# Experts: the fourth gated product's turn, cast and split, placed ahead of the third pair's down-products and of the next block's first weight half

## What is computed

```python
def clamped_swiglu(g, u):
    g = jnp.minimum(g, SWIGLU_LIMIT)
    u = jnp.clip(u, -SWIGLU_LIMIT, SWIGLU_LIMIT)
    return g * jax.nn.sigmoid(SWIGLU_ALPHA * g) * (u + 1)

def expert_block(args):
    xb, e = args                       # 128 rows of one expert
    hid = xb @ w1[e] + b1[e]           # 1024 -> 2 x 1024
    return clamped_swiglu(hid[:, :D_FF_3], hid[:, D_FF_3:]) @ w2[e] + b2[e]

ys = lax.map(expert_block, (xs, blk_e)).reshape(-1, D)
```

## Time and profile before

| what | value |
|---|---|
| median of 3 runs | 3641.12 us (3632.57 to 3645.83) |
| span of the profiled execution | 3646.2 us |
| busy, share of the span | TensorE 90%, its weight loads 69%, VectorE 62%, ScalarE 43%, GpSimd 7% |
| expert blocks | about 2443 us to 3600 us of the span |

### The profile page before, as it was taken

One profiled execution on the slowest core, in us unless ns is written; L12 is line 12 of the kernel. 1 busy time (PEld: TensorE's weight loads), 2 busy tenths in 40 slices (PEclk: granted clock), 3 DMA queues, 4 the chain that ended last, 5 costly groups with the idle time before them and its releaser, 6 DMA issues. The chain is left out here.

```text
span 3646.2 us, 47903 instructions
## 1 busy us (share of the span) xinstructions
PE 3284.8 (90%) x17130; PEld 2526.6 (69%) x17130; DVE 2265.7 (62%) x2932; ACT 1553.7 (43%) x1964; POOL 266.3 (7%) x194
## 2 busy tenths in 40 slices
PE   7888999999988878899987877869999999999996
PEld 5655787875447557788755655758888888888885
DVE  4375666335703264554445474468888888888885
ACT  1263332010012641200123053247777777777773
POOL 0000000000000000000000000002122212122211
PEclk9889999999989887899988988979999999999997
DMA  5411222232112000122273201069999999999994
GB/s 163 155 30 35 92 92 90 95 93 93 69 36 68 14 1 11 61 95 95 84 283 118 81 5 40 28 254 409 399 373 381 371 381 371 383 368 384 368 385 164
DMA packets 170827, 639.66 MB, mean 175 GB/s; under 512 B 13242, under 2 KB 89146, under 8 KB 113875
## 3 DMA queue, kind: packets, MB, share of 16 engines
q1 hardware_dynamic: 160434, 599.53, 43.6%
q0 software_dynamic: 9648, 35.13, 3.6%
q10 hardware_dynamic: 624, 3.35, 0.2%
HBM read 610.12 MB, written 30.46 MB: 176 GB/s over the span
## 5 line engine op out<-in xcount | busy, mean ns | idle before, releaser
L500 DVE TENSOR_TENSOR experts_rest<-experts_weights,experts_leading 128x2048 fp32r<-128x2048 f32 x386 | 879.2, 2285 | 87.2 <-ACT experts_leading L3118 85.8
L3118 ACT CAST experts_leading<-experts_weights 128x2048 fp32r<-128x2048 f32 x387 | 728.5, 1904 | 31.0 <-PEq L3108 16.9
L506 PE MATMUL psum<-experts_leading,experts_xT_leading 128*128 128x512 f32 x1024 | 402.7, 393 | 7.7 <-DVE experts_rest L500 7.7
L507 PE MATMUL psum<-experts_rest,experts_xT_leading 128*128 128x512 f32 x1024 | 404.7, 395 | 0.0
L508 PE MATMUL psum<-experts_leading,experts_xT_rest 128*128 128x512 f32 x1024 | 403.2, 394 | 0.0
L506 PEld LDWEIGHTS psum<-experts_leading,experts_xT_leading 128*128 128x128 f32 x1024 | 192.9, 188 | 52.6 <-DVE experts_rest L500 8.1
L507 PEld LDWEIGHTS psum<-experts_rest,experts_xT_leading 128*128 128x128 f32 x1024 | 193.1, 189 | 44.6
L508 PEld LDWEIGHTS psum<-experts_leading,experts_xT_rest 128*128 128x128 f32 x1024 | 193.0, 188 | 43.4
L506 PE MATMUL psum<-experts_leading,experts_hidden_leading 128*128 128x512 f32 x512 | 211.4, 413 | 3.4 <-DVE experts_hidden_rest L3204 3.3
L507 PE MATMUL psum<-experts_rest,experts_hidden_leading 128*128 128x512 f32 x512 | 201.4, 393 | 0.0
L508 PE MATMUL psum<-experts_leading,experts_hidden_rest 128*128 128x512 f32 x512 | 200.7, 392 | 0.0
(11 more groups left out here) (756 smaller groups left out, 6849.9 us busy)
## 6 DMA issues: line engine op xcount, KB each, us to landing
experts_weights<-in_w_up SPq DMA_DIRECT2D x259, 1024.0 KB, 9.6
experts_weights<-in_w_down SPq DMA_DIRECT2D x128, 1024.0 KB, 6.4
ada_unit<-in_w_ada SPq DMA_DIRECT2D x12, 2048.0 KB, 18.2
merge_first<-in_w_merge SPq DMA_DIRECT2D x16, 768.0 KB, 4.4
merge_weights<-in_w_merge SPq DMA_DIRECT2D x16, 768.0 KB, 4.1
ff_up_first<-in_w_up SPq DMA_DIRECT2D x11, 1024.0 KB, 4.8
ff_up_weights<-in_w_up SPq DMA_DIRECT2D x11, 1024.0 KB, 4.7
down_first<-in_w_down SPq DMA_DIRECT2D x8, 704.0 KB, 4.8
```

The costliest lines, as they stand in the source:

```text
L500: return dve.tensor_tensor(out, src, leading.bitcast(F32), ALU.subtract)
L506: pe.matmul(out, lh, rh, start=start, stop=False)
L507: pe.matmul(out, lh, rl, start=False, stop=False)
L3118: act.copy(leading[h % LEADING], weights.half(h)).then_inc(masked, 1)
```

## The change

It moves one call in each of three engines' lists. On TensorE, the turn of product 3 is issued after down(9) and before down(10) with pair 2, where it stood behind it. On ScalarE, the cast of hidden pair 3 is issued before the cast of the next block's half 0, where it stood behind it. On VectorE, the split of hidden pair 3 is issued before the split of the next block's half 0. No instruction, buffer, semaphore or transfer is added or removed.

```diff
@@ TensorE
                     down(9, (0, 1)).then_inc(consumed, 1)
+                    turn_product(3, b * UNITS + 3)
                     down(10, (2,))
-                    turn_product(3, b * UNITS + 3)
                     down(11, (2,))
@@ ScalarE
                     mask_hidden(2)
+                    mask_hidden(3)
                     mask(0, b + 1)
-                    mask_hidden(3)
                     mask(1, b + 1)
@@ VectorE
                     split_half(11, b)
+                    split_hidden(3)
                     split_half(0, b + 1)
-                    split_hidden(3)
                     split_x(1 - s, i + s)
```

## The result

The changed kernel takes 3652.73 us (median of 15 runs, 3643.06 to 3658.48), the kernel before 3643.13 us (15 runs, 3632.57 to 3647.70). The forecast of the difference was +9.7 us.

A forecast was written before the change was run, and what follows sets the result against it. TensorE was taken as the bound, busy 1096.8 of 1100 us at full clock in the expert blocks. 16 x 0.21 + 15 x 0.44 - 0.24 = +9.7 us, so 3641.1 becomes 3650.8 us; range 3637 to 3662.

The forecast's parts named there:

- The pauses of before: TensorE's waits for hidden pair 3 at down(10, (3,)): 0.47 and 0.24 us in alternate blocks, 11.4 us in all, would go.
- The chain: Turn of product 3 (T), hidden cast, half 0 cast and split, split_x: next bias matmul at T + 6.35, TensorE due T + 5.75.
- The restart: From split_x's end to the next block's bias matmul: 0.15 us plus 0.14 for three TensorE sequencer steps, bounds 0 and 0.30.
- the even case: Block border: sequencer steps cost nothing and restart takes 0.12 us, so old and new waits cancel; +4.4, about 3642 us; 22%.
- The sum: All block borders: 16 of one kind at +0.21 us, 15 of the other at +0.44, last block -0.24; total +9.7 us.
- Behind that: After the delayed split_x, in the next block's halves 1 to 3: no further loss booked.
- The cover: Room before TensorE wants the next block's half 1, after the delayed split_x: 1.2 us.
- Only the pauses go: Faster rival: split_x on time at the block border, chain at most 5.75 us, minus 11.4 us to 3629.7; 4%.
- The dear restart: Slower rival: TensorE's sequencer waits after the block-border stall cost 0.3 us more per border, +19, 3660 us; 14%.
- The clock rival: Slower rival: pauses at block borders leave three matmuls each at the lower clock, adding 19 us, 3669 us; 2%.

The follow-up runs named there:

- experiment 1: The changed kernel with split_x also moved ahead of the next block's split_half(0) on VectorE; 3631.54 us against 3640.86 for the kernel before, ratio 0.9979.
- Experiment 2: The changed kernel with only ScalarE's edit undone; 3632.54 us against 3640.86 for the kernel before, ratio 0.9979.
- Experiment 6: The changed kernel with TensorE's wait for split_x put last of the waits ahead of a block's first bias matmul; 3646.20 us, ratio to before 1.0013.
- experiment 7: The changed kernel with an added VectorE fill of 1024 unused columns between split_half(0) and split_x; 3683.09 us, ratio to before 1.0110.
- experiment 9: The changed kernel with only VectorE's edit undone; 3738.60 us against 3642.62 for the kernel before, ratio 1.0270.
- experiment 4: The kernel before with VectorE's edit alone; 3651.02 us against 3640.86 for the kernel before, ratio 1.0025.

## Why the prediction was right

*The pauses of before.* Right as places. As a prize they were over-sized, a term of the sum that came out smaller: the kernels of experiments 1 and 2 have no pause at all and need 71.95 us for a pair of blocks, 0.60 less than before's 72.55, where 0.47 + 0.24 = 0.71 was booked. Over the stretch from the first to the last border that is 9.1 us instead of 10.7 (30 borders), and the timed difference of experiment 1 is 9.3 us. TensorE's own steps came out 0.11 us a pair longer than the rows of before gave. They are in no one place: an ordinary step is 0.2309 us on average in the kernel before and 0.2312 in the changed kernel and in experiments 1 and 2, and a pair has some 285 of them. Why, is open.

*TensorE's and ScalarE's edits.* As worked out: the turn came 1.38 us earlier with respect to its surroundings, the hidden cast 0.42 behind it, the next cast 0.28 behind that. Experiment 2 shows that ScalarE's edit is the part that does the harm.

*The chain.* Forecast T + 6.35 for the bias matmul, measured T + 6.34 and T + 6.39 at the two kinds of border. Its links: cast of half 0 seen through by VectorE at T + 2.63 (2.65), split_x ended at T + 6.06 (6.06). TensorE due at T + 5.75, measured in experiment 1 at T + 5.77.

*The restart.* Chosen 0.15 + 0.14 = 0.29 between bounds of 0.15 and 0.45; measured 0.29 and 0.34. Experiment 6 shows that the choice for "the steps count" over the even case was right: with these steps out of the way the kernel is at +3.6 us against before, near the 4.4 of the even case. How the term was put together was not right, and its size is partly luck: the steps cost 0.10 to 0.14 us each and not their recorded 0.04 to 0.05, there are two or three of them, and the 0.15 of the old pause already holds one.

*The sum.* +9.7 forecast, +9.6 and +9.7 measured. That it is so near is partly luck. The interval of the measurement is +7 to +12 us, and the profiled executions give +11.1 us for the 30 blocks between the borders, 0.75 for a pair (73.30 against 72.55) where 0.65 was forecast. The new pauses came out as booked: 0.80 - 0.23 + 0.08 = 0.65 us and, at the other kind of border, 0.70, where 0.68 was booked for both. What was missed is the 0.11 us a pair by which the old ones were worth less, 1.7 us in all.

*Behind that.* No long step inside the up-products; VectorE's wait before half 2 is gone. The cover held. ScalarE's idle time before the hidden cast is 2.6 us where some 2.4 was forecast.

*Rivals.* "Only the pauses go" needed split_x in time for TensorE at T + 5.75; it is what experiments 1 and 2 are, and there the section Optimization Strategy of the Trainium skill's Perfetto Trace Analysis is right: what the gap waited for was made to start sooner, and with nothing long put between the turn and split_x this gave the gain. In the changed kernel the gap moved instead. The dear restart didn't come: 0.08 behind the wait, as before. The clock rival didn't come at pauses of 0.6 us, nor of 1.6 (experiment 7), but did at 2.4 us (experiment 9), in every second block. The Trainium skill, TensorE: Matmul & The Clock Gate, section A second HAM failure mode, tells of a kernel whose clock swings between its two levels because TensorE is idle for short times between groups of matmuls; experiment 9 agrees, with its 2.4 us, and the kernels with the shorter pauses show no such swing.

## What to carry to other kernels

When an instruction that waits is moved ahead of one that doesn't on an in-order engine, add up what is queued behind it until the next thing that the bound engine wants, from the moment at which its wait ends; the other engine's order decides whether the time saved is kept. Here a cast of 1.9 us and a split of 2.3 were put in series behind a late event, and the cure was to fill the wait with work that was ready, or to leave the long cast where it was. The last wait in front of the bound engine should be the one that ends last: each step behind it is paid, here with 0.10 to 0.14 us.

## What the runs showed of the hardware

Each sequencer step of TensorE that stood behind the deciding wait cost 0.10 to 0.14 us, though each is recorded with 0.04 to 0.05 us. From the end of the VectorE instruction to the matmul it was 0.05 us with no such step and 0.15 with one (experiment 6), 0.24 to 0.29 with two and 0.34 with three (the changed kernel and experiment 4).

Pauses of TensorE of 0.6 us and of 1.55 to 1.64 us, one in each block of 37 to 38 us, left the granted clock at 1.00; pauses of 2.4 us in each block brought it to 0.50 for some 3 us in every second block, at a cost of about 1.4 us each.
